# The masked score jobs of a gated linear attention in blocks of 64 by 64 in place of 32 by 32

## What is computed

```
diff = b[:, :, :, None, :] - b[:, :, None, :, :]
decay = jnp.exp(jnp.where(causal[:, :, None], diff, -jnp.inf))
scores = jnp.einsum('bhtd,bhsd,bhtsd->bhts', qi, ki, decay)
intra = jnp.einsum('bhts,bhse->bhte', scores, vi)
```

## Time and profile before

| | |
|---|---|
| median of 3 runs | 1033.16 us (1033.12 to 1034.02) |
| profiled execution | 1033.45 us |
| its span | 1031.4 us |
| TensorE busy | 1023.3 us, 99% |
| TensorE weight loads | 989.7 us, 96% |
| VectorE busy | 604.4 us, 59% |
| ScalarE busy | 490.3 us, 48% |
| GpSimd busy | 270.3 us, 26% |

### The profile page before, as it was taken

One profiled execution on the slowest core, in us unless ns is written; L12 is line 12 of the kernel. 1 busy time (PEld: TensorE's weight loads), 2 busy tenths in 40 slices (PEclk: granted clock), 3 DMA queues, 4 the chain that ended last, 5 costly groups with the idle time before them and its releaser, 6 DMA issues.

```text
span 1031.4 us, 21175 instructions
## 1 busy us (share of the span) xinstructions
PE 1023.3 (99%) x8894; PEld 989.7 (96%) x8894; DVE 604.4 (59%) x580; ACT 490.3 (48%) x541; POOL 270.3 (26%) x184
## 2 busy tenths in 40 slices
PE   9999999999999999999999999999999999999997
PEld 8999999989999999999999999999899999999886
DVE  5744554488967645454386545543889676555452
ACT  6544343456556534444454443434565565434331
POOL 0333330123402333330113333301234023433200
PEclk9999999999999999999999999999999999999999
DMA  9765536635336655435746553366453347565621
GB/s 295 243 196 169 154 116 195 215 123 165 125 91 196 196 173 181 148 112 174 231 133 208 187 176 127 113 199 215 123 165 126 125 161 241 168 202 188 197 84 41
DMA packets 162323, 172.10 MB, mean 167 GB/s; under 512 B 8621, under 2 KB 149193, under 8 KB 162265
## 3 DMA queue, kind: packets, MB, share of 16 engines
q1 hardware_dynamic: 161816, 170.92, 52.3%
q10 hardware_dynamic: 448, 0.34, 0.1%
HBM read 170.18 MB, written 1.05 MB: 166 GB/s over the span
## 4 chain that ended last, share of the span: by engine, by line
PE 98%; DVE 1%; ACT 0%; issue 0%; DVEq 0%
PE ps L1278 24%; PE ps L1280 24%; PE ps L1279 24%; PE ps L1398 3%; PE ps L1310 2%; PE ps L1295 2%; PE ps L1311 2%; PE ps L1440 2%; PE ps L1482 2%; PE ps L1480 2%; PE ps L1481 2%; PE ps L1441 2%; PE ps L1509 1%; PE ps L1627 1%; PE ps L1410 1%; PE ps L1337 1%
## 5 line engine op out<-in xcount | busy, mean ns | idle before, releaser
L766 DVE TENSOR_TENSOR w_lo<-raw,w_hi 128x2048 fp32r<-128x2048 f32 (+3 forms) x175 | 384.5, 2200 | 297.6 <-ACT w_hi L507 297.1
L1278 PE MATMUL ps<-x_hi,w_hi 128*128 128x272 f32 (+2 forms) x1568 | 449.9, 287 | 0.1
L1279 PE MATMUL ps<-x_lo,w_hi 128*128 128x272 f32 (+2 forms) x1568 | 448.9, 286 | 0.0
L1280 PE MATMUL ps<-x_hi,w_lo 128*128 128x272 f32 (+2 forms) x1568 | 448.7, 286 | 0.0
L507 ACT ACTIVATE w_hi<-raw 128x2048 fp32r<-128x2048 f32 (+3 forms) x175 | 312.9, 1791 | 208.5 <-PE ps L1280 155.5
L1278 PEld LDWEIGHTS ps<-x_hi,w_hi 128*128 128x128 f32 x1568 | 295.3, 188 | 1.8 <-issue 1.2
L1279 PEld LDWEIGHTS ps<-x_lo,w_hi 128*128 128x128 f32 x1568 | 295.1, 188 | 0.1
L1280 PEld LDWEIGHTS ps<-x_hi,w_lo 128*128 128x128 f32 x1568 | 294.8, 188 | 0.0
L1196 POOL TENSOR_TENSOR up<-gate,up 128x544 f32<-128x544 f32 (+1 forms) x44 | 59.4, 1351 | 315.4 <-ACT gate L591 315.4
L1199 POOL TENSOR_TENSOR hid_lo<-up,hid_hi 128x544 f32 (+3 forms) x44 | 122.3, 2779 | 46.5 <-ACT hid_hi L595 46.5
L591 ACT ACTIVATE gate<-gate 128x544 f32<-128x544 f32 (+1 forms) x44 | 28.7, 653 | 200.0 <-DVE gate L933 200.0
(11 more groups left out here) (206 smaller groups left out, 1134.2 us busy)
## 6 DMA issues: line engine op xcount, KB each, us to landing
raw<-in_ffn_wg SPq DMA_DIRECT2D x87, 512.0 KB, 4.0
raw<-in_ffn_wu SPq DMA_DIRECT2D x87, 512.0 KB, 4.9
raw<-in_ffn_wd SPq DMA_DIRECT2D x72, 384.0 KB, 3.2
raw<-in_w_in SPq DMA_DIRECT2D x40, 512.0 KB, 4.6
raw<-in_ffn_wd SPq DMA_DIRECT2D x20, 512.0 KB, 4.7
raw<-in_w_out SPq DMA_DIRECT2D x16, 512.0 KB, 4.5
raw<-in_ffn_wd SPq DMA_DIRECT2D x28, 256.0 KB, 3.2
x_tok<-in_x SPq DMA_DIRECT2D x4, 256.0 KB, 4.6
```

What stands on the lines that cost most here:

```text
L766: v_.tensor_tensor(w_lo[:, slot, 0:n], raw[:, slot, 0:n], f32(w_hi[:, slot, 0:n]), ALU.subtract)\
L1278: pe.matmul(out_, wh, xh, start=first, stop=False)
L1279: pe.matmul(out_, wh, xl, start=False, stop=False)
L1280: return pe.matmul(out_, wl, xh, start=False, stop=last)
```

## The change

The masked jobs compute 16 blocks of 64 keys by 64 queries each in place of 32 of 32 by 32. The masks are laid out for 64 columns: in the rows of either half, the 32 columns that are on the diagonal hold the old mask and the others zeros, so that what enters s_c outside the diagonal stays at the zeros of the clearing. s_c has 64 columns per group, and the masked copy goes over 512 elements per partition in place of 256. ScalarE reads the 32 wanted columns out of 64. The tails keep their blocks of 32 by 16, written behind the wider scores in the bank, and get masks of their own (tail_mask). The constants grow by 4 x 32 + 3 x 16 = 176 columns. The midpoints (mid), which had a place of their own, now lie in the second half of z_pad, which is free at that time. In job, the loop over block positions s0 now stands outside the loop over row halves r, for jobs 4 and 5 too.

```diff
-    c = np.zeros((P, P + 2 * T + MASKED * 32), np.float32)
+    c = np.zeros((P, P + 2 * T + MASKED * 64 + TAILED * (T - 2 * P)), np.float32)
...
     s, t = np.arange(P)[:, None] % 32, np.arange(32)[None, :]
+    masks = [(s // BASE == t // BASE) & (s <= t)]
+    for bs in LEVELS:
+        masks.append((s // bs == t // bs) & (s % bs < bs // 2) & (t % bs >= bs // 2))
     at = P + 2 * T
-    c[:, at:at + 32] = (s // BASE == t // BASE) & (s <= t)
-    for n, bs in enumerate(LEVELS):
-        at += 32
-        c[:, at:at + 32] = (s // bs == t // bs) & (s % bs < bs // 2) & (t % bs >= bs // 2)
+    for m in masks:
+        for o in range(0, P, 32):
+            half = at + o % 64
+            c[o:o + 32, half:half + 32] = m[o:o + 32]
+        at += 64
+    for m in masks[:TAILED]:
+        c[:, at:at + T - 2 * P] = m[:, 32 - (T - 2 * P):]
+        at += T - 2 * P
...
-        s_c = place("s_c", [P, 2, 4, 32])
+        s_c = place("s_c", [P, 2, 4, 64])
...
-        mid = place("mid", [P, 2, T // BASE])
         z_pad = place("z_pad", [P, 2, 2 + T])
+        mid = z_pad[:, 1, 2:2 + 2 * T // BASE].rearrange("p (a n) -> p a n", a=2)
...
                         last = act.activation(s_all[o:o + 32, :, :, o:o + 32].rearrange("p c (a r) t -> p r (c a) t", r=2),
-                                              s_c[o:o + 32], ACT.Copy)
+                                              s_c[o:o + 32, :, :, o % 64:o % 64 + 32], ACT.Copy)
...
-                        src = ps[:, bank:bank + 2, 0:P].rearrange("p r (g t) -> p r g t", g=4)
+                        src = ps[:, bank:bank + 2, 0:4 * 64].rearrange("p r (g t) -> p r g t", g=4)
...
                         last = v_.copy_predicated(
-                            s_c[:, :, :, :], mask(j, P, 32).unsqueeze(1).unsqueeze(1).to_broadcast([P, 2, 4, 32]), src)
+                            s_c[:, :, :, :], mask(j).unsqueeze(1).unsqueeze(1).to_broadcast([P, 2, 4, 64]), src)
                         if j < TAILED:
                             last = v_.copy_predicated(
-                                s_last[:, :, :], mask(j, P, 32)[:, TAIL:32].unsqueeze(1).to_broadcast([P, 2, TAIL]),
-                                ps[:, bank:bank + 2, P:P + TAIL])
+                                s_last[:, :, :], tail_mask(j).unsqueeze(1).to_broadcast([P, 2, TAIL]),
+                                ps[:, bank:bank + 2, 4 * 64:4 * 64 + TAIL])
...
                                 o, g = ch * P, 2 * ch + a
-                                for r in range(2):
-                                    if j < MASKED:
-                                        for s0 in range(0, P, 32):
-                                            sl = slice(o + s0, o + s0 + 32)
-                                            last = score(s0, 32, r, 32 * g, a, sl, sl)
-                                    elif j < JOBS - 2:
-                                        bs = 2 * BASE << (j - 1)
-                                        hf = bs // 2
-                                        for s0 in range(0, P, bs):
+                                if j < MASKED:
+                                    bs, hf = 64, 64
+                                elif j < JOBS - 2:
+                                    bs = 2 * BASE << (j - 1)
+                                    hf = bs // 2
+                                else:
+                                    bs = hf = P
+                                for s0 in range(0, P, bs):
+
+                                    for r in range(2):
+                                        if j < MASKED:
+                                            sl = slice(o + s0, o + s0 + bs)
+                                            last = score(s0, bs, r, bs * g, a, sl, sl)
+                                        elif j < JOBS - 2:
                                             mid_ = o + s0 + hf
                                             last = score(s0, hf, r, hf * g, a, slice(mid_ - hf, mid_),
                                                          slice(mid_, mid_ + hf))
...
                             if j < TAILED:
 
                                 for r in range(2):
-                                    last = score(32 * (2 * a + r), 32, r, P, a, slice(T - 32, T), slice(2 * P, T))
+                                    last = score(32 * (2 * a + r), 32, r, 4 * 64, a, slice(T - 32, T), slice(2 * P, T))
```

More of the change, by code:

```diff
@@ L137, in trunk @@
         w_lo = sb("w_lo", [P, RING, UNIT], F32R)
-        cst = sb("cst", [P, P + 2 * T + MASKED * 32])
+        cst = sb("cst", [P, P + 2 * T + MASKED * 64 + TAILED * TAIL])
         w_glow = sb("w_glow", [P, DEPTH * KT, NMETA])
@@ L154, in trunk, with mask, tail_mask @@
                                                 for i in range(4))
-        def mask(n, rows, cols):
-            at = P + 2 * T + n * 32
-            return cst[0:rows, at:at + cols].bitcast(U32)
+        def mask(n):
+            at = P + 2 * T + n * 64
+            return cst[:, at:at + 64].bitcast(U32)
+        def tail_mask(n):
+            at = P + 2 * T + MASKED * 64 + n * TAIL
+            return cst[:, at:at + TAIL].bitcast(U32)
         ffn_floats = 2 * FT * T + 8 * T
         PAD = 16
-        mix_floats = (6 * 2 + 4 * 4 + 2 * HEADS + 4 + 2 + 8) * T + 1536 + 8 * 32 + 4 * TAIL + 2 * (2 + T) + 2 * T // BASE
+        mix_floats = (6 * 2 + 4 * 4 + 2 * HEADS + 4 + 2 + 8) * T + 1536 + 8 * 64 + 4 * TAIL + 2 * (2 + T)
         arena_bytes = 4 * max(ffn_floats, mix_floats)
@@ L1643, in job @@
                                                          slice(mid_, mid_ + hf))
[L1644 to L1647, removed]
+                                        elif j == JOBS - 2 and ch == 0:
+                                            last = score(0, P, r, P * a, a, slice(0, P), slice(P, 2 * P))
+                                        elif j == JOBS - 1:
+                                            last = score(0, P, r, TAIL * g, a, slice(o, o + P), slice(2 * P, T))
                             if j < TAILED:
                                 for r in range(2):
-                                    last = score(32 * (2 * a + r), 32, r, P, a, slice(T - 32, T), slice(2 * P, T))
+                                    last = score(32 * (2 * a + r), 32, r, 4 * 64, a, slice(T - 32, T), slice(2 * P, T))
                         last.then_inc(job_mm, 1)
```

## The result

| | before | after |
|---|---|---|
| median, first nine runs each | 1033.16 us (1032.77 to 1034.02) | 1035.85 us (1034.51 to 1036.61) |
| ratio, 95% interval | | 1.0025 [1.0016, 1.0034] |
| median, second set | 1033.31 us (33 runs) | 1035.47 us (11 runs) |
| ratio, 95% interval | | 1.0019 [1.0010, 1.0028] |
| span of the profiled execution | 1031.4 us | 1033.2 us |

The change made the kernel slower, by 2.7 us in the first set and 2.2 in the second. Prediction: +1.7, range 1032.5 to 1036.6.

What follows compares the result with a forecast made beforehand. TensorE's matmul stream was taken as the bound. Six jobs with tails (+1.9 us) and job 3 twice (-0.16) made +1.7, other engines 0, so 1033.16 + 1.7 = 1034.9 us, range 1032.5 to 1036.6.

Steps and rivals of the forecast that it cites:

- What bounds the kernel: TensorE's matmul stream in the two mixers: no other engine is late, so a microsecond on or off goes one for one.
- Small tiles: Job 3, masked without tail: 8 rounds of 0.053 us on 2 x 2 positions, 0.61 for 0.69, -0.16 in all.
- rival 2: 64-wide blocks on TensorE: column halves don't run side by side, +0.43 us a job, 1038.3 us; chance 0.08.
- Rival 3: Masked score jobs on TensorE: instructions set the pace all the way, -2.6 us, 1030.6 us; chance 0.07.
- The shape changes: Jobs 0 to 2: three more tile-shape changes around the tails, 0.39 us a job; net +0.31 taken, six times +1.9.
- load time counted twice: Shape price in jobs 0 to 2: if all double, a change costs 0.09 to 0.10 us, +0.27 a job.
- Rival 1: Tails in jobs 0 to 2: their change of shape costs nothing, -0.3 us, 1032.9 us; chance 0.18.
- VectorE: Masked copies on VectorE: +0.3 us each, eight times, covered by its lead over TensorE, so 0 in the time.
- The wait in front of g0: Second mixer, g0 projection behind yq_lo: tightest lead, 1.37 us; about +0.9 of VectorE lateness fits, so no wait.

Runs made afterwards that it cites:

- the grouped product: Kernel before, with the product of scores and values reordered: 128-row matmuls of all four heads first, then the four 32-row ones; 1029.93 us, ratio 0.9971.
- copies_only: Changed kernel's copies, masks, constants and layout, but masked jobs on TensorE again 32 blocks of 32x32; 1033.38 us, ratio 1.0004 to the kernel before.

## Why the prediction was right

- **What bounds the kernel.** TensorE's stream, one for one, held for a stream that gets longer: +1.96 by the jobs, +2.00 in the two mixers. The span's +1.8 is that, 0.2 between the mixers, and a job 0 that began 0.41 earlier in this execution. It held less for one that gets shorter: job 5's queries have 0.30 us of lead in the second mixer. I read the end of a merged row for jobs 5 and 6 together (270.47 against job 6) and passed over job 5 itself. It cost nothing here, because the change is a lengthening.
- **Small tiles.** 8 rounds of 0.053 for job 3: 0.61 foreseen, 0.62 measured. Row halves and column halves run side by side for 64x64 blocks too, so rival 2 (1038.3) is out. Rival 3 is out as well: 40 records took longer than 72.
- **The shape changes.** This was the term that decides, and its mechanism is shown from four sides: one change in place of three (0.81 for 1.12), none (the time of before), three in the kernel before (+1.85 us), and the grouped product. That the price of a change of rows would hold for a change of column width was an assumption behind which no row stood; I allowed anything from nothing to the full price and took a middle value, so that it came out this close is in part luck. Its size was a little too small: I took +0.31 a job, measured +0.35, which is my own upper reading of the same rows (+0.36). What I took off for load time counted twice should have stayed in. This is the mis-sized term: 6 x 0.04 = 0.24 us; with it, and 0.02 less gained on job 3, the sum of +1.7 is the +1.96 measured.
- **Rival 1** (a width change within 64 rows costs nothing) is out by the same runs. No row before had shown such a change, and I had left it 0.18.
- **VectorE.** 0.29 more per masked copy for 0.3 taken, no wait of TensorE, and in the time nothing beyond the 0.2 between the mixers that stays open (copies_only). The wait in front of g0 that I called the tightest didn't come: yq_lo was done at 792.87, g0 began at 794.63, a lead of 1.76 where it had been 1.37. The wider copies didn't make VectorE late here; it moved by 1.38 and TensorE by 1.77.

```profile
792.01 0.86 DVE L1109 SCALAR_TENSOR_TENSOR yq_lo<-ps,par,yq_hi 128x256 fp32r<-128x256 f32 x2
...
794.63 0.39 PE L1290 MATMUL ps<-x_hi,w_hi 128*128 128x256 f32 x1
```

- **The number.** 1034.9 forecast, 1035.85 and 1035.47 measured, inside the range. The mechanism gives +1.96; the sets gave +2.7 and +2.2, whose intervals (+1.6 to +3.5, +1.0 to +2.9) both hold it. The 0.2 between the mixers comes on top of it; no term of mine had it. Whether anything more of the first set's +2.7 is other than spread stays open.
- **The chances.** I gave "within 0.2%" 0.57 and "slower" 0.35. The result lies on the bound between them: both ratios' intervals hold 1.002. With a forecast 0.4 us from the bound and the price's upper reading at +2.0, half and half would have been the fair reading of my own rows. Two bounds there don't follow from the working: the +1.0 as the forecast's lower end (the sum's own was -0.3), and 1036.6 as its upper (1033.16 + 3.3 is 1036.5). Neither decides anything.

## What to carry to other kernels

Count the changes of tile shape in TensorE's stream, not only its matmuls: halving the matmuls lost 2 us here because the blocks no longer had the shape of the short ones between them. Where a loop over heads mixes two shapes, put all matmuls of one shape first; 3 us came from one reordered loop that nobody had asked about. Before counting on a shorter stream, look for the smallest lead of each job's operands, one by one and in every repetition of the stage.

## What the runs showed of the hardware

A change of the column width alone, 64 to 32 and back with 64 rows on both sides, costs time like a change of rows: the first with all short records made 0.19 us over job 3, the two others, with the tails in two groups, 0.31 more. With 128 rows on both sides a change from 32 to 16 active columns showed nothing: the glow products kept the pace of the sum of squares ahead of them. Four short matmuls on four row positions take the time of one (0.34 for 0.32 us), so of the two placements run here, a lone narrow pair between wide ones was the dearer by far.
